# A mixture-of-experts encoder step: the last stage's sums and norms moved into the expert loop, as running sums in device memory

## The reference, cut to what matters

```python
h = x + mixed @ w_out
idx, wts = hier_route(rmsnorm(h, norm_ffn), ...)     # 2 of 32 experts for each token
y = h + sum over the 2 of  wts * ((silu(r @ wg[e]) * (r @ wu[e])) @ wd[e])    # r = rmsnorm(h)
out = y * rsqrt(mean(y * y) + 1e-6) * norm_final
```

## Time and profile before

| what | us |
|---|---|
| median of three runs (lowest, highest) | 1813.04 (1806.34, 1813.47) |
| the profiled execution's own time | 1812.19 |
| its span, first to last instruction | 1810.5 |
| TensorE busy | 1760.3 (97%) |
| VectorE busy | 1047.7 (58%) |
| ScalarE busy | 860.7 (48%) |
| GpSimd busy | 118.8 (7%) |

### The profile page before, as it was taken

The page is one execution under the profiler, slowest core; times in us unless marked ns, Lnnn a source line. Parts: engine busy times, 40 slices in busy tenths (PEclk is TensorE's granted clock), DMA queues, the critical chain, the costliest instruction groups (busy, mean ns, idle before and its releaser), DMA issues.

```text
span 1810.5 us, 25543 instructions
## 1 busy us (share of the span) xinstructions
PE 1760.3 (97%) x10346; PEld 1562.7 (86%) x10346; DVE 1047.7 (58%) x1303; ACT 860.7 (48%) x1093; POOL 118.8 (7%) x139
## 2 busy tenths in 40 slices
PE   8999999999999999999999999989999999999995
PEld 7888888988898899999999988878888888888872
DVE  5347775433445431223243255678989998898965
ACT  4225554331543331211122223268887878788863
POOL 0010000000000020000000000010000000000024
PEclk9999999999999999999999999989999999999997
DMA  5241111112122132222221232189999999999987
GB/s 189 85 120 30 31 32 37 35 32 60 35 64 83 41 98 64 88 63 83 70 99 47 76 146 71 65 331 403 419 408 417 414 413 415 414 415 415 415 290 262
DMA packets 140762, 329.42 MB, mean 182 GB/s; under 512 B 15978, under 2 KB 92646, under 8 KB 115941
## 3 DMA queue, kind: packets, MB, share of 16 engines
q1 hardware_dynamic: 123764, 272.25, 40.7%
q0 software_dynamic: 12128, 38.74, 5.9%
q10 hardware_dynamic: 4752, 16.78, 2.3%
HBM read 290.09 MB, written 39.87 MB: 182 GB/s over the span
## 4 chain that ended last, share of the span: by engine, by line
PE 61%; DVE 1%; DMA 1%; DVEq 0%; issue 0%; ACT 0%; ACTq 0%; POOLq 0%
PE banks L72 7%; PE banks L70 7%; PE banks L71 7%; PE banks L2233 6%; PE banks L2235 6%; PE banks L2234 6%; PE banks L2261 3%; PE banks L2259 3%; PE banks L2260 3%; PE banks L2112 2%; PE banks L2114 2%; PE banks L2113 2%; PE banks L2219 2%; PE banks L2243 1%; PE banks L2142 1%; DMA yb<-expert_rows,sidx 1%
## 5 line engine op out<-in xcount | busy, mean ns | idle before, releaser
L2732 DVE TENSOR_TENSOR low<-raw,hig 128x2048 fp32r<-128x2048 f32 x192 | 431.4, 2285 | 58.0 <-ACT hig L2434 55.6
L2434 ACT ACTIVATE hig<-raw 128x2048 fp32r<-128x2048 f32 x192 | 359.3, 1916 | 20.8 <-ACT ye L2507 14.5
L2233 PE MATMUL banks<-hig,xel 128*128 128x512 f32 x512 | 203.1, 397 | 0.2 <-DVE xel L2804 0.2
L2235 PE MATMUL banks<-hig,xeh 128*128 128x512 f32 x512 | 200.2, 391 | 0.0
L2234 PE MATMUL banks<-low,xeh 128*128 128x512 f32 x512 | 199.8, 390 | 0.0
L70 PE MATMUL banks<-xhi,glo 128*128 128x384 f32 (+1 forms) x552 | 180.0, 326 | 1.9 <-PEq L65 1.9
L72 PE MATMUL banks<-xhi,ghi 128*128 128x384 f32 (+1 forms) x552 | 180.0, 326 | 0.0
L71 PE MATMUL banks<-xlo,ghi 128*128 128x384 f32 (+1 forms) x552 | 179.9, 326 | 0.0
L70 PE MATMUL gproj<-xhi,glo 128*128 128x384 f32 (+1 forms) x384 | 130.1, 339 | 0.0
L72 PE MATMUL gproj<-xhi,ghi 128*128 128x384 f32 (+1 forms) x384 | 125.4, 326 | 0.0
L71 PE MATMUL gproj<-xlo,ghi 128*128 128x384 f32 (+1 forms) x384 | 125.2, 326 | 0.0
(11 more groups left out here) (484 smaller groups left out, 3510.9 us busy)
## 6 DMA issues: line engine op xcount, KB each, us to landing
raw<-in_w_e_gate_dram SPq DMA_DIRECT2D x64, 1024.0 KB, 8.1
raw<-in_w_e_up_dram SPq DMA_DIRECT2D x64, 1024.0 KB, 8.2
raw<-in_w_e_down_dram SPq DMA_DIRECT2D x64, 1024.0 KB, 7.5
graw<-in_w_in_dram SPq DMA_DIRECT2D x39, 512.0 KB, 3.8
expert_rows<-ye ACTq DMA_DIRECT2D x31, 512.0 KB, 8.3
xt<-in_x_prompt_dram SPq DMA_DIRECT2D x16, 512.0 KB, 3.6
expert_rows<-nil POOLq DMA_DIRECT2D x16, 512.0 KB, 4.0
braw<-in_w_branch_dram SPq DMA_DIRECT2D x24, 256.0 KB, 3.0
```

The lines of the kernel that those rows point to most:

```text
L2233: nc.tensor.matmul(bank[:, :], xel[n % 2][:, kk, :], wh[:, k, :], start=(kk == 0), stop=False)
L2235: last = nc.tensor.matmul(bank[:, :], xeh[n % 2][:, kk, :], wh[:, k, :], start=False, stop=(kk == KC - 1))
L2434: nc.scalar.activation(hig[q % HI][:, :], raw[q % RAW][:, :], ACT.Copy).then_inc(high, 1)
L2732: nc.vector.tensor_tensor(low[q % RAW][:, :], raw[q % RAW][:, :], hig[q % HI][:, :].bitcast(F32), ALU.subtract).then_inc(lowed, 1)
```

## The change

There are no expert rows in device memory any more. A tensor `acd` (`sum_rows`) holds one running sum per token and starts as h, stored by GpSimd next to the normed rows. Each slot gets a row of eight integers, `meta`: the token; its weight; and three places that are either a row or far out of bounds: where the running sum goes back (only if the token's other expert is still to come), and where the finished row goes in the prompt's or the sample's output (only if this expert is the token's second). VectorE works this table out in turns 0 and 1 of the expert loop instead of 8, 11 and 14. GpSimd scatters it in 18 indirect DMAs to device memory by slot and loads it back as tiles, ahead of its expert loop.

Per expert c GpSimd then gathers the rows of expert c+4, waits until ScalarE has copied expert c out to one of three `ye` buffers (now scaled by the weight; GpSimd scales the first three), gathers the running sums onto them with an adding DMA, normalises expert c-1, and scatters expert c's sums back. Each adding gather waits until the scatter of the expert before has landed. The normalising (`finish`) multiplies by the final gain, makes the inverse root in integer and float steps on one column, scales, and scatters the rows twice (prompt and sample). ScalarE squares expert n-2 in turn n, once its sums have been added. Gathers and scatters skip places out of bounds, and an empty slot is out of bounds. The last three experts are finished by VectorE and ScalarE. The overflow blocks are rewritten in the same way. The clearing of overflow rows (L1987) goes.

```diff
             for t in range(NT):
                 r = rows_of(t)
                 pool.wait_ge(ndone, t + 1)
                 pool.dma_start(htd[t * P:t * P + r, :], nrow[t % 2][0:r, :]).then_inc(kept[t % 2], 16)
+                pool.dma_start(wide(acd[t * P:t * P + r, :]), hrow(t, r)).then_inc(hkept, 16)
...
+            def sum_rows(n, dst, compute):
+                pool.wait_ge(low_out, 16 * n)
+                pool.indirect_dma_start(dst[:, :], None, acd, bass.IndirectOffsetOnAxis(ap=toks[:, n:n + 1], axis=0),
+                                        bounds_check=T - 1, oob_is_err=False, compute_op=compute).then_inc(hr_in, 16)
+
+            def finish(c):
+                pool.wait_ge(squared, c + 1)
+                ms, x, y, u = stat[:, c:c + 1], root[:, 0:1], root[:, 1:2], root[:, 2:3]
+                if c >= 2:
+                    pool.wait_ge(y_out[c % 2], 32 * (c // 2))
+                nc.gpsimd.tensor_tensor(yo[c % 2][:, :], ye[c % YE][:, :], gf[:, :], ALU.mult)
+                nc.gpsimd.tensor_scalar(x, ms, EPS, None, ALU.add)
+                pool.drain()
+                nc.gpsimd.tensor_copy(u, x.bitcast(I32))
+                pool.drain()
+                nc.gpsimd.tensor_scalar(u, u, -0.5, 1597463007.0, ALU.mult, ALU.add)
+                pool.drain()
+                nc.gpsimd.tensor_copy(y.bitcast(I32), u)
+                pool.drain()
+                for _ in range(3):
+                    nc.gpsimd.tensor_scalar(u, y, y, x, ALU.mult, ALU.mult)
+                    pool.drain()
+                    nc.gpsimd.tensor_scalar(u, u, -0.5, 1.5, ALU.mult, ALU.add)
+                    pool.drain()
+                    nc.gpsimd.tensor_scalar(y, y, u, None, ALU.mult)
+                    pool.drain()
+                nc.gpsimd.tensor_scalar(yo[c % 2][:, :], yo[c % 2][:, :], y, None, ALU.mult).then_inc(scaled, 1)
+                pool.wait_ge(scaled, c + 1)
+                out_rows(pool, yo[c % 2], meta[:, c, :], y_out[c % 2])
...
+            x_rows(2)
+            x_rows(3)
+            pool.wait_ge(filled, 16)
             pool.wait_ge(found, 1)
-            pool.wait_ge(s0, 16 * (LATE // P // 2))
-            pool.wait_ge(s1, 16 * (LATE // P // 2))
-            pool.wait_ge(used, spent("u", NE - 2, 1))
-            for t in TAIL:
+            for t in range(NT):
                 r = rows_of(t)
...
+                for k in range(2):
+                    pool.indirect_dma_start(slot_meta, bass.IndirectOffsetOnAxis(ap=sidx[k][0:r, t:t + 1], axis=0),
+                                            smeta[0:r, t, k, :], None).then_inc(meta_out, 16)
+            pool.wait_ge(meta_out, 16 * 2 * NT)
+            for n0, n1, arrived in ((0, 4, meta_in0), (4, NE, meta_in1)):
+                pool.dma_start(meta[:, n0:n1, :], slot_meta[n0 * P:n1 * P, :].rearrange("(n p) e -> p n e", p=P)).then_inc(arrived, 16)
+            pool.wait_ge(norm_in, 16)
+            for c in range(NE - 2):
+                if c + 4 < NE:
+                    x_rows(c + 4)
+                if c == 0:
+                    pool.wait_ge(meta_in0, 16)
+                if c == 4:
+                    pool.wait_ge(meta_in1, 16)
+                pool.wait_ge(emptied, c + 1)
+                if c < YE:
+                    nc.gpsimd.tensor_scalar(ye[c][:, :], ye[c][:, :], share(c), None, ALU.mult).then_inc(shared, 1)
+                    pool.wait_ge(shared, c + 1)
+                sum_rows(c, ye[c % YE], ALU.add)
+                if c:
+                    finish(c - 1)
+                pool.wait_ge(hr_in, 16 * c + 16)
+                low_rows(pool, ye[c % YE], meta[:, c, :], low_out)
+            c = NE - 2
+            sum_rows(c, hr, ALU.bypass)
+            pool.wait_ge(joined, 1)
+            low_rows(pool, ye[c % YE], meta[:, c, :], low_out)
+            sum_rows(c + 1, hr, ALU.bypass)
...
             def out(n):
-                if n >= 2:
-                    act.wait_ge(stored[n % 2], 16 * (n // 2))
+                if n >= YE:
+                    act.wait_ge(scaled, n - YE + 1)
+                    act.wait_ge(low_out, 16 * (n - YE + 1))
                 act.wait_ge(used, place["d", n, 1] + 1)
...
+            def square(c):
+                if c < NE - 2:
+                    act.wait_ge(hr_in, 16 * c + 16)
+                else:
+                    act.wait_ge(joined, 1)
+                nc.scalar.activation(junk[:, :], ye[c % YE][:, :], ACT.Square, scale=D ** -0.5,
+                                     accum_out=stat[:, c:c + 1]).then_inc(squared, 1)
...
                     split_high(q0 + 4)
                     split_high(q0 + 5)
                     silu(n)
+                if 2 <= n < NE:
+                    square(n - 2)
                 if n == 0:
                     x_high(1)
                 elif n < NE:
...
-                if n in (8, 11, 14):
-                    (overflow, order, slots)[(n - 8) // 3]()
+                if n == 0:
+                    overflow()
+                    ve.drain()
+                    order()
+                    ve.drain()
+                if n == 1:
+                    slots()
```

More of the change, by code:

```diff
@@ L2455, in _ @@
             w_high(LEAD + 2)
-            act.wait_ge(cleared, 16 * OVER)
             sigmoid(LEAD + 1)
@@ L2907, in _, with last_scale @@
                     split_low(q0 + 9)
-                if n in (8, 11, 14):
-                    (overflow, order, slots)[(n - 8) // 3]()
+                if n == 0:
+                    overflow()
+                    ve.drain()
+                    order()
+                    ve.drain()
+                if n == 1:
+                    slots()
+            c = NE - 2
+            ve.wait_ge(emptied, c + 1)
+            ve.wait_ge(hr_in, 16 * c + 16)
+            nc.vector.tensor_tensor(ye[c % YE][:, :], ye[c % YE][:, :], hr[:, :], ALU.add).then_inc(joined, 1)
+            ve.wait_ge(norm_in, 16)
+            def last_scale(i):
+                c = NE - 3 + i
+                ve.wait_ge(rootd, i + 1)
+                nc.vector.scalar_tensor_tensor(out=last_yo[i][:, :], in0=ye[c % YE][:, :], scalar=stat[:, 32 + c:33 + c],
+                                               in1=gf[:, :], op0=ALU.mult, op1=ALU.mult).then_inc(last_scaled, 1)
+            for i in range(2):
+                ve.wait_ge(y_out[1 - i], 32 * ((NE - 3 + i) // 2))
+                last_scale(i)
+            c = NE - 1
+            ve.wait_ge(hr_in, 16 * c + 16)
+            ve.wait_ge(scaled, c - YE + 1)
+            ve.wait_ge(low_out, 16 * (c - YE + 1))
+            for half in range(2):
+                cols = slice(512 * half, 512 * half + 512)
+                if half == 0:
+                    ve.wait_ge(lefthalf, 1)
+                else:
+                    ve.wait_ge(used, len(halves))
+                last = nc.vector.scalar_tensor_tensor(out=ye[c % YE][:, cols], in0=[PA, PB][half][:, :], scalar=share(c),
+                                                      in1=hr[:, cols], op0=ALU.mult, op1=ALU.add).then_inc(parted, 1)
+            ve.wait_ge(parted, 2)
+            ve.sem_inc(emptied, 1)
+            ve.wait_ge(part_sq, 1)
+            nc.vector.tensor_scalar(part_ms[:, 1:2], part_ms[:, 0:1], EPS, None, ALU.add).then_inc(eps_added, 1)
+            last_scale(2)
             def body(b, e):
@@ L2939, in _ @@
-            for j, t in enumerate(ON_PE):
-                for k in range(2):
-                    last = nc.vector.tensor_scalar(dg[:, 2 * j + k, :], ident[:, :], wts[:, t, k:k + 1], None, ALU.mult)
-            last.then_inc(diagonal, 1)
-            for t in TAIL[:AHEAD]:
-                if t in ON_DVE:
-                    add_lower(t)
-            ve.drain()
-            ve.wait_ge(norm_in, 16)
-            for i in range(NT - 1):
-                if TAIL[i] in ON_DVE:
-                    add_upper(TAIL[i])
-                if i + AHEAD < NT and TAIL[i + AHEAD] in ON_DVE:
-                    add_lower(TAIL[i + AHEAD])
-                    ve.drain()
-                if i >= 2:
-                    scale(TAIL[i - 2])
@@ L2956, in _ @@
-            t = TAIL[-1]
-            ve.wait_ge(ya_in[t], 32)
-            for half in range(2):
-                c = slice(512 * half, 512 * half + 512)
-                nc.vector.scalar_tensor_tensor(out=ya[t][:, c], in0=ya[t][:, c], scalar=wts[:, t, 0:1],
-                                               in1=yb[t][:, c], op0=ALU.mult, op1=ALU.add).then_inc(part_sum, 1)
-            scale(TAIL[-3])
-            ve.wait_ge(part_square, 1)
-            nc.vector.tensor_scalar(stat[:, 48:49], stat[:, 48:49], EPS, None, ALU.add).then_inc(eps_added, 1)
@@ L2965, in _ @@
-            scale(TAIL[-2])
-            ve.wait_ge(inverted, NT)
-            for half in range(2):
-                c = slice(512 * half, 512 * half + 512)
-                nc.vector.scalar_tensor_tensor(out=yo[t][:, c], in0=ya[t][:, c], scalar=stat[:, 32 + t:33 + t],
```

(4 more changed lines are left out.)

339 lines of the change are left out of this document (128 added, 211 removed).

## The result

| | before | after |
|---|---|---|
| median of 4 runs, us | 1813.16 (1806.34 to 1813.47) | 2282.22 (2273.10 to 2283.18) |
| ratio after / before | | 1.2596, 95% interval 1.2573 to 1.2619 |
| profiled execution, us | 1812.19 | 2273.10, span 2271.5 |
| forecast, us | | 2008, range 1860 to 2140 |

Slower, as forecast, but by 469 us and not by 196; the time lies outside the range. The forecast had three parts, and each can be read from the profile after.

The account below looks back on a forecast made before the run. TensorE bounded the kernel before, at 17.75 us a beat; GpSimd's serial chain was to bound the changed one. 1275 at the start + 29 beats x 24.2 + 29.7 end + 1.7 outside the span = 2008 us, range 1860 to 2140.

Parts of the forecast that it names:

- The start: Before expert 1's down product: TensorE waits for slot table and expert 0's adding gather, costing 40 us, 35 to 50.
- The end: From expert 29's running-sum scatter: device-memory round trips 18.9, then last sums to store and a second scatter, 29.7 in all.
- VectorE, ScalarE and the DMA engines as the bound: Expert loop, rivals: one of these engines sets the beat, giving 1912, 1878 or 1930 us; chance 0.22 together.
- a hidden loop: Expert loop, rival: all minima hold, 17.6 under TensorE's 17.75, only the start stall left, 1825 us; chance 0.09.
- not slower: Slot table, rival: scatters issue at half the gathers' pitch or less and the loop is hidden, 1812 us; chance 0.04.
- The beat: GpSimd's chain: Expert loop: GpSimd's serial work per expert sets the beat, 6.0 + 1.9 + 16.3 = 24.2 us, ends 17.6 and 36.
- Its own landing lies beside the normalising: Expert loop: the adding gather's landing runs beside the normalising; only its issue and gaps, 1.9 us, count in the beat.
- Scaling: Normalising on GpSimd: scaling 1024 columns takes 1.0 us, priced as the 1088-column fill.
- VectorE's splits: Normalising: 15 GpSimd operations that read each wait about 0.6 in half of the cases, 5.0 us added to the beat.
- The steps: Normalising on GpSimd: 13 one-column steps with a drain behind each, 0.4 a step, 5.2 us.
- The scatter's landing: Expert loop: the next adding gather waits for the running-sum scatter to land, taken as 6.0 us.
- GpSimd is slower still: Expert loop, rival: every operation meets a split, or drains cost 0.7; beat of 29, 2147 us; chance 0.15.

Follow-up runs that it names:

- e4: Changed kernel with each of the 18 slot-table scatters issued twice, the second to a table nobody reads: 2307.43 us.
- e1: Changed kernel without the normalising of experts 0 to 28, their rows scattered straight from ye, every DMA kept: 1998.03 us.
- e5: Changed kernel with the first four drains of each normalisation made semaphore waits, the nine of the Newton steps kept: 2226.12 us.
- e9: Changed kernel with all 13 drains of each normalisation made semaphore waits, order and work unchanged: 2084.42 us.
- e10: e9 with the running-sum scatter issued behind the steps and ahead of the scaling of the expert before: 2055.00 us.
- e3: Changed kernel with VectorE's weight splits cut from 2048 to 16 columns, TensorE reading the high half instead of the low: 2164.89 us.
- e7: e1 with ScalarE's square one turn later, expert n-3 instead of n-2 in turn n: 1903.26 us.
- e2: Changed kernel with the running-sum scatter issued inside the normalising of the expert before, behind its first Newton step: 2277.83 us.
- e6: Changed kernel with the edits of e2 and e3 together: 2101.32 us.
- e8: Changed kernel with one Newton step instead of three in each normalisation: 2188.65 us.
- e11: e10 with ScalarE's square one turn later, expert n-3 in turn n: 2052.19 us in 4 runs, 1.1335 times the kernel before.

## Why the prediction was wrong

**The start** was right to 2 us (1275.80 after 1277.5), and e4 shows that it is paid in full. The number is better than its terms, which offset: the last table scatter landed at 1258.9 and not at 1263.3, and from there to the gather's landing passed 14.5 us and not 11.7, as the scaling of expert 0's rows took 2.88 where 1.2 was taken. What the start left out is that the first beat behind the stall is 20 us longer.

**The end** was right, 29.8 for 29.7, and here too two terms offset: up to the last sums 17.4 us after 18.9, from there on 12.4 after 10.8.

**That GpSimd's chain sets the beat** was right. e1, e5, e9 and e10 take parts from that chain alone, and the time follows each of them. Of the rivals, VectorE, ScalarE and the DMA engines as the bound fall with the stretch table (50, 46 and 63% busy); a hidden loop and "not slower" fall with the beat.

**The beat: GpSimd's chain** is the step that failed, and in it the sentence "Its own landing lies beside the normalising". The prediction had one landing in the beat, the scatter's; there are two. It priced a drain by rows of small operations, 0.12 us each and once 1.46, where no indirect transfer was on its way, so these rows could not show what a drain behind a gather waits for. With the drains gone (e9) the sentence comes true, and the beat falls by 6.6 us to 26.8, which is within the 22 to 27 of the forecast. Not all of the 9.2 us is this step's, though. The wait itself is 2.4 a beat; e9 gives back more, as the steps then run ahead of VectorE's splits, a term that the forecast had priced. The rest of the miss are terms of the sum that were too small.

These are, by size, and with them the terms that held:
- Scaling: 1.2 taken, 3.7 without VectorE (e3). The row chosen was a fill of 1088 columns, which reads nothing; the scaling took 2.88, and 0.84 passed from its end to the scatter behind it. The 128x512 subtraction, from which the product had been worked out, was the nearer row, and gave 2.3.
- VectorE's splits: 5.0 taken (15 operations, 0.6 us in half the cases, make 4.5), 6.9 measured (after less e3). The mechanism was named; left out was that the issue of an indirect transfer is held as well (2.49 in the mean for the first output scatter in the kernel after, 1.08 in e3). The trace of before had a sign of it, in the view of tile xe, whose landing line is the earlier trace rows: in the expert loop the issue of a gather took 0.95 us with no split beside it, 1.37 in the median, mostly ending 0.8 behind the end of a split, and 3.0 at the most. So "1.0 for every gather whatever was queued" was a misreading. The row has the least, median and greatest ns:

```profile
L2021 POOL DMA_INDIRECT xe<-ffn_rows,toks x32: 947/1372/2998, 1185.9 to 1699.4; - x32
```

- The steps: 5.2 taken, 5.05 in e3 without the first of the 13. Right.
- The scatter's landing: 6.3 with the gap, 8.1 measured.

The rival "GpSimd is slower still" (29 us, 2147 us) named drains at 0.7 as a cause. In fact one drain is long and twelve are short, 0.17 in the mean, and the time lies beyond that rival too. The ends that the prediction gave its own sum, 17.6 and 36, do hold the 33.4; its range stopped at a beat of 29.

That the stage would bring little even with a perfect chain is argued from e7 alone: two landings in a row, 20.3 us, against 17.75. No run shows the chain with both landings short.

## What to carry to other kernels

Before a step is hidden beside a transfer, look at every instruction of that step: a drain on GpSimd behind its own indirect transfer takes the landing onto the chain (2.4 to 6.4 us a beat here), a semaphore on the one instruction that is meant does not. And ask what else that landing releases, since work that is made to wait for it then runs side by side with it. A landing is priced at the traffic that will run beside it, and that traffic comes back as soon as the beat shortens, so the gain of a repair is measured together with it. And an engine that stands idle may be where another's exclusive work was hidden: filling the gap of e2 gave nothing, as VectorE's splits only moved onto other instructions.

## What had not been expected of the hardware

- A drain on GpSimd ends 0.3 us behind the landing of the indirect gather issued before it (24 of 29 beats within 0.01), and in e6 0.2 us behind the landing of an indirect scatter (28 of 29). In e9 semaphore waits between small operations cost 0.06 to 0.11 us each, less than the drains' 0.17 in the mean.
- VectorE's splits hold the issue of an indirect transfer on GpSimd: the first output scatter took 2.49 us in the mean beside them and 1.08 without (e3).
- Without VectorE's splits (e3) a 128x1024 product took GpSimd 2.93 us and a 128x1024 scaling by one column's value 2.88: the second wide operand cost it 0.05.
- The adding gather, of 68 rows in the mean, landed in 6.1 us with 0.17 MB of other transfers beside it, and in 10.5 to 12.1 in the median of the runs in which it met the weight loads (e3, e8 to e11).
